# An SSM batch on one Trainium2 core: turning the B products inside unit 1 and making the V products inside unit 2

## The chip, the core and the metric

The kernel runs on one NeuronCore of a Trainium2 chip. Its engines are TensorE (PE, matmuls and transposes), VectorE (DVE), ScalarE (ACT), GpSimd (POOL) and SyncE (SP, which here issues DMAs). The metric is the device time of one execution in microseconds (us), lower being better. The kernel before takes 2384.48 us, the median of 3 runs.

## What is computed

One inference step of a two-layer trunk, in float32. Layer 0 projects 640 tokens (512 of a prompt, 8 streams of 16) to 4096 columns, runs a diagonal state space model (SSM, "S5") over 96 groups of 16 columns on a part of them, attends to a memory with another part, and projects back. Layer 1 does the same with stick-breaking attention in place of the SSM. Only the SSM matters here:

```python
hn = rms_norm(x, g_pre)
u, gate, mq, mg = _split_proj(hn @ w_in)          # the projection that the SSM is interleaved with
y, h_last = s5_scan(u.reshape(bsz, l, SSM_GROUPS, SSM_GROUP), h0, ...)
# in s5_scan, per group:
bu = einsum('gph,btgh->btgp', b_bar, u_blk)       # inputs to the 64 complex states of a group
_, h_loc = lax.associative_scan(_ssm_combine, (a, bu), axis=1)
hs = h_loc + pows[None] * h_prev[:, None]
y = real(einsum('ghp,btgp->btgh', cmat, hs)) + d32 * u_blk
```

## The kernel before

**The projection.** `w_in` is consumed in 16 chunks of 256 columns, each in 4 units. A unit is 4 blocks of 128 rows of the weight; TensorE makes it in four quarters (`q` = 0 to 3 of `unit_stationary`: two blocks of columns by two halves of the tokens), each 4 times the three matmuls of lines 206 to 208, into PSUM banks 0 to 3. The weights of a unit come by DMA into `RAW`, ScalarE rounds them to the high part `WH` (`split_high`, line 174) and VectorE makes the low part `WL` from both (`split_low`, line 188). There are four slots; ScalarE and VectorE split unit U+2 when they stand at unit U (`ahead`), and a slot is loaded again when TensorE is done with its unit.

**The SSM batch.** Chunks 1 to 12 are made in a hardware loop of 6 iterations. One iteration is one SSM batch: 8 units (x = 0 to 7) and, between them, the SSM work for 16 groups (8 pairs). Each engine runs its own instructions in the written order, so a wait holds everything that stands behind it. In a batch the steps are:

- `turn_c` (TensorE, line 483, ahead of unit 0) turns the C matrices and the states; it waits until VectorE has made the last of the three additions of the batch before (`late`, line 712).
- `tables` with `input_products` (VectorE, after its split at unit 0, lines 648 to 380) makes `BV`, the B matrices times powers of A; the semaphore is `s_bv`.
- `second` (ScalarE, line 591) copies a part of `BV` to `BB`.
- `turn_bv` (TensorE, line 496) turns `BV` with 16 transposes into banks 4 to 7. `copy_wv` (ScalarE, line 598) copies them to `WV`.
- `products_v` (TensorE, line 508) makes the V products, inputs of the scan, from `WV` and `U`, in two parts of 16 small matmuls. `copy_v` (ScalarE, line 606) copies each part to `W` and signals `s_Ve`.
- `products_lags` (TensorE, line 521, ahead of unit 4).
- `first`, `second`, `third`, `fourth` of `ssm_dve` (VectorE, lines 633 to 701, one behind each of its splits at x = 3 to 6) run the scan over 64 columns in six levels, then the streams, and write `HPZ`; the semaphore is `s_hp`. `first` waits for both parts of `s_Ve`.
- `products_y` (TensorE, after unit 7): 16 matmuls on `TZ` (line 531), the wait for `s_hp`, 16 matmuls on `HPZ` (line 536), two transposes (line 542). VectorE adds the three banks to `YS` (line 712, `s_ye`); the next batch's `turn_c` waits for the last.

The lists that set the order are `aux` in `ssm_pe` for TensorE and the lists that `ssm_act` and `ssm_dve` return, whose entry k is run behind the split at unit k (entry 8 after the batch). SyncE's and GpSimd's programs hold the stores of `YS` and the loads of `U` that `copy_v` and `products_v` wait for.

Of the kernel before, what the change touches and what calls it, by code (L numbers as in the profile page):

```python
# [76 lines left out]
def build(nc, io, out, scr):  # L77
# [13 lines left out]
    with ExitStack() as ctx:  # L91
# [43 lines left out]
        at = 0  # L135
# [341 lines left out]
        def ssm_pe(pe, ph, i):  # L477

            def turn_c():
                pe.wait_ge(s_crd, i * 80 + 80)  # L480
                pe.wait_ge(s_ye, i * 3 + 3)
                for k in range(2):
                    pe.transpose(PS[:, 4, k * P:k * P + P], CR[:, k, :], ident[:])
                for k in range(2):
                    ins = pe.transpose(PS[:, 4, 256 + 64 * k:320 + 64 * k],
                                       SR[0:64, :].rearrange("b (m r) -> b r m", r=2)[:, k, :], ident[0:64, 0:64])
                ins.then_inc(s_cT, 1)

            def turn_bv():
                pe.wait_ge(s_bv, i + 2)  # L490
                pe.wait_ge(s_cTe, i + 1)
                pe.wait_ge(s_fTe, i + 1)
                for x in range(4):
                    for j in range(4):
                        r, jj = x // 2, 4 * (x % 2) + j
                        ins = pe.transpose(PS[:, 4 + x, j * P:j * P + P], BV[:, r, jj].rearrange("p s h -> p (s h)"), ident[:])
                ins.then_inc(s_wvT, 1)

            def products_v(part):
                if part == 0:  # L500
                    pe.wait_ge(s_u, i * 128 + 128)
                    pe.wait_ge(s_wve, i * 4 + 4)
                for a in range(2):
                    for j in range(4):
                        jj = 4 * part + j
                        for q in range(2):
                            c = j * NC
                            ins = pe.matmul(PS[q * ST:q * ST + ST, 4 + 2 * a + part, c:c + NC],
                                            WV[:, (a * JB + jj) * P + q * ST:(a * JB + jj) * P + q * ST + ST], U[:, 2 * jj + q, :],
                                            start=(j == 0), stop=True, skip_group_check=True)  # L510
                ins.then_inc(s_V, 1)

            def products_lags():
                pe.wait_ge(s_cp, i + 2)
                pe.wait_ge(s_bb, i + 2)
                pe.wait_ge(s_Ve, i * 2 + 2)
                for a in range(2):
                    for r in range(2):
                        for x in range(4):
                            j = 4 * a + x  # L520
                            ins = pe.matmul(PS[32 * x:32 * x + 32, 4 + a, 0:P], BB[:, r, j].rearrange("p q h -> p (q h)"),
                                            CP[:, r, j, 0:8].rearrange("p k h -> p (k h)"),
                                            start=(r == 0), stop=(r == 1), skip_group_check=True)
                ins.then_inc(s_kd, 1)

            def products_y():
                pe.wait_ge(s_tz, i * 128 + 128)
                pe.wait_ge(s_kde, i + 2)
                for g in range(2 * JB):
                    o = PS[:, 4 + g // 6, (g % 6) * NC:(g % 6 + 1) * NC]  # L530
                    pe.matmul(o, TZ[:, g, :], U[:, g, :], start=(g % 6 == 0), stop=False, skip_group_check=True)
                pe.wait_ge(s_hp, i + 2)
                for j in range(JB):
                    o = PS[:, 4 + j // 3, (j % 3) * 2 * NC:(j % 3 + 1) * 2 * NC].rearrange("p (q c) -> p q c", q=2)
                    for r in range(2):
                        ins = pe.matmul(o, CP[:, r, j, 1:9].rearrange("p k h -> p (k h)"), HPZ[:, r, :, j, :],  # L536
                                        start=False, stop=(r == 1), skip_group_check=True)
                    if j in (2, 5, 7):
                        ins.then_inc(s_y, 1)
                pe.wait_ge(s_fs, i + 1)  # L540
                for r in range(2):
                    ins = pe.transpose(PS[0:72, 7, r * P:r * P + P], FS[:, r].rearrange("p b j -> p (b j)"), ident[:])
                ins.then_inc(s_fT, 1)

            aux = {0: [turn_c], 2: [turn_bv], 3: [lambda: products_v(0)], 4: [products_lags]}
            for x in range(8):
                for f in aux.get(x, ()):
                    f()
                n = i * 2 + 1 + x // 4
                unit_stationary(pe, ph, (i * 2 + 1 + x // 4) * 4 + ph.first + x % 4, x % 4, n,  # L550
                                (lambda q: products_v(1) if q == 2 else None) if x == 3 else None)
            products_y()

        def ssm_sync(sp, i):
# [19 lines left out]
        def ssm_act(act, mine, i):  # L574

            def early():
                act.wait_ge(s_cT, i + 2)
                act.wait_ge(s_cp, i + 1)
                act.wait_ge(s_hp, i + 1)
                act.activation(CTH[:, 0:P], PS[:, 4, 0:P], ACT.Copy)  # L580
                act.activation(CTH[:, P:2 * P], PS[:, 4, P:2 * P], ACT.Copy, scale=-1.0)
                act.activation(CTH[:, 2 * P:384], PS[:, 4, 2 * P:384], ACT.Copy).then_inc(s_cTe, 1)

            def second():
                act.wait_ge(s_zero, 3)

                act.wait_ge(s_bv, i + 2)
                act.wait_ge(s_kd, i + 1)
                for q in range(2):
                    r = slice(q * ST, q * ST + ST)  # L590
                    ins = act.activation(BB[r, :, :, q, :], BV[r, :, :, STEPS - 1, :], ACT.Copy)
                ins.then_inc(s_bb, 1)

            def copy_wv():
                act.wait_ge(s_wvT, i + 2)
                for x in range(4):
                    act.activation(WV[:, x * 512:(x + 1) * 512], PS[:, 4 + x, :], ACT.Copy).then_inc(s_wve, 1)

            def copy_v():  # L600
                for part in range(2):
                    act.wait_ge(s_V, i * 2 + 1 + part)
                    if part == 0:
                        act.wait_ge(s_yst, i * 128 + 128)
                    for a in range(2):
                        ins = act.activation(W[:, a, 4 * part:4 * part + 4, :],
                                             PS[:, 4 + 2 * a + part, 0:4 * NC].rearrange("p (j c) -> p j c", j=4), ACT.Copy)
                    ins.then_inc(s_Ve, 1)

            def lags():  # L610
                act.wait_ge(s_kd, i + 2)
                act.wait_ge(s_kst, i * 16 + 16)
                act.activation(KDS[:], PS[:, 4:6, 0:P], ACT.Copy).then_inc(s_kde, 1)

            def late():
                act.wait_ge(s_fT, i + 2)
                act.wait_ge(s_fst, i * 32 + 32)
                act.activation(FO[0:72, :].rearrange("b (m r) -> b r m", r=2),
                               PS[0:72, 7, 0:2 * P].rearrange("b (r m) -> b r m", r=2), ACT.Copy).then_inc(s_fTe, 1)

            return [early, second, copy_wv, copy_v, lags, None, None, None, late]

        def ssm_dve(dve, mine, i):

# [826 lines left out]
        def _(pe):  # L1451
# [40 lines left out]
            with pe.Fori(0, BATCHES) as i:  # L1492
                ssm_pe(pe, ph, i)
# [88 lines left out]
        def _(act):  # L1582
# [75 lines left out]
            with act.Fori(0, BATCHES) as i:  # L1658
                aux = ssm_act(act, mine, i)
                chunk("in_a", i * 2 + 1, i + 1, aux[0:4])  # L1660
                chunk("in_a", i * 2 + 2, i + 10, aux[4:8])
                aux[8]()
# [519 lines left out]
```

## Time and profile before

| | |
|---|---|
| median of 3 runs | 2384.48 us (2380.51 to 2387.82) |
| the profiled execution | 2382.36 us |
| its span | 2380.7 us |
| TensorE busy | 2270.9 us (95%) |
| VectorE, ScalarE, GpSimd busy | 1015.0, 872.3, 290.7 us |
| the loop of 6 SSM batches | from about 155 to 605 us of the span |

Times in the rows below are microseconds from the start of the span. A timeline row has the start, how long the group lasted, the engine, line, operation, what it writes and reads, and how many instructions; in brackets stands how long the engine had been idle before it and who ended the wait.
### The profile page before, as it was taken

To read this page: it belongs to the slowest core of one execution; us is meant where nothing else is said; L and a number is where in the kernel's file an instruction comes from. 1 tells how busy PE (TensorE), PEld (TensorE's weight loads), DVE (VectorE), ACT (ScalarE), POOL (GpSimd) and SP (SyncE) were. 2 spreads that over 40 slices of the span, in tenths; PEclk is the share of its full clock that TensorE was granted. 3 is DMA by queue.
4 is the path that set the end of the run, shared out by engine and by line. 5 is a ranking of instruction groups with operands and counts; after the bars stand their busy time and mean duration, and the time that the engine had idled before them with its cause. 6 is when DMAs were issued, how large, how long until landed. Compare 5 with 4: busy or idle time off the path is not lost.

```text
span 2380.7 us, 36018 instructions
## 1 busy us (share of the span) xinstructions
PE 2270.9 (95%) x13890; PEld 2042.3 (86%) x13890; DVE 1015.0 (43%) x1775; ACT 872.3 (37%) x1596; POOL 290.7 (12%) x580
## 2 busy tenths in 40 slices
PE   8999999999799999999999999999999999889997
PEld 6799999999788998887888889888988888878886
DVE  5658888988534362225222221222212223543223
ACT  4542333323345352224222223544455444442221
POOL 1422120220101000002000000121121211010001
PEclk9999999999899999999999999999999999999998
DMA  7634433433534334223233234334343345244223
GB/s 258 220 81 114 109 103 91 118 102 104 202 117 140 107 105 160 79 80 150 93 102 101 94 100 135 109 107 150 98 139 108 111 147 205 88 151 160 79 79 133
DMA packets 177834, 293.45 MB, mean 123 GB/s; under 512 B 25524, under 2 KB 105056, under 8 KB 174304
## 3 DMA queue, kind: packets, MB, share of 16 engines
q1 hardware_dynamic: 132720, 159.32, 22.3%
q0 software_dynamic: 24304, 88.99, 12.0%
q10 hardware_dynamic: 20736, 44.11, 5.1%
q8 instruction: 51, 0.84, 0.1%
q14 instruction: 23, 0.19, 0.0%
HBM read 243.75 MB, written 48.61 MB: 123 GB/s over the span
## 4 chain that ended last, share of the span: by engine, by line
PE 76%; DVE 9%; DMA 5%; issue 4%; ACT 4%; POOL 1%; ACTq 0%; SPq 0%; POOLq 0%; DVEq 0%
PE PS L1349 11%; PE PS L1351 11%; PE PS L1350 11%; PE PS L206 10%; PE PS L208 10%; PE PS L207 10%; DMA FA<-in_cache_k_dram 2%; DVE WL L188 2%; PE PS L536 2%; DVE FA L643 1%; PE PS L1131 1%; DVE FA L639 1%; PE PS L793 1%; DVE FA L634 1%; PE PS L1116 1%
## 5 line engine op out<-in xcount | busy, mean ns | idle before, releaser
L206 PE MATMUL PS<-XH,WH 128*128 128x320 f32 x2336 | 741.3, 317 | 4.9 <-ACT EST L1639 2.1
L207 PE MATMUL PS<-XL,WH 128*128 128x320 f32 x2336 | 724.9, 310 | 0.0
L208 PE MATMUL PS<-XH,WL 128*128 128x320 f32 x2336 | 724.9, 310 | 0.0
L188 DVE SCALAR_TENSOR_TENSOR WL<-RAW,vec,WH 128x256 fp32r<-128x256 f32 (+1 forms) x608 | 283.6, 527 | 631.8 <-ACT WH L174 627.3
L1349 PE MATMUL PS<-WH,XH 128*128 128x512 f32 x1168 | 456.7, 391 | 7.6 <-DVE WL L183 4.5
L1351 PE MATMUL PS<-WH,XL 128*128 128x512 f32 x1168 | 455.4, 390 | 0.0
L1350 PE MATMUL PS<-WL,XH 128*128 128x512 f32 x1168 | 455.3, 390 | 0.0
L206 PEld LDWEIGHTS PS<-XH,WH 128*128 128x128 f32 x2336 | 442.0, 189 | 13.7 <-issue 5.9
L207 PEld LDWEIGHTS PS<-XL,WH 128*128 128x128 f32 x2336 | 442.0, 189 | 3.1 <-issue 2.9
L208 PEld LDWEIGHTS PS<-XH,WL 128*128 128x128 f32 x2336 | 441.4, 189 | 0.0
L174 ACT ACTIVATE WH<-RAW,vec 128x256 fp32r<-128x256 f32 (+1 forms) x608 | 281.4, 532 | 374.9 <-DMA RAW<-in_w_kv_dram 177.0
L183 DVE TENSOR_TENSOR WL<-RAW,WH 128x1024 fp32r<-128x1024 f32 (+1 forms) x120 | 141.6, 1182 | 339.4 <-ACT WH L170 339.1
L1349 PEld LDWEIGHTS PS<-WH,XH 128*128 128x128 f32 x1168 | 220.0, 188 | 54.6 <-DVE WL L183 5.7
L1351 PEld LDWEIGHTS PS<-WH,XL 128*128 128x128 f32 x1168 | 219.7, 188 | 45.9
L1350 PEld LDWEIGHTS PS<-WL,XH 128*128 128x128 f32 x1168 | 220.0, 188 | 45.6
L170 ACT ACTIVATE WH<-RAW 128x1024 fp32r<-128x1024 f32 (+1 forms) x120 | 121.6, 1016 | 337.2 <-DMA RAW<-in_w_out_b_dram 132.3
L1639 ACT ACTIVATE EST<-PS 128x320 f32<-128x320 f32 x116 | 49.8, 439 | 126.5 <-PE PS L208 126.0
L1177 POOL TENSOR_SCALAR_AFFINE_SELECT FA<-FA 128x128 f32<-128x128 f32 x120 | 30.5, 291 | 364.8 <-DVE FA L1243 246.3
L1445 POOL TENSOR_SCALAR rstd<-ss 128x1 f32<-128x1 f32 x20 | 5.9, 296 | 479.6 <-DVE ss L1931 396.5
L1243 DVE SCALAR_TENSOR_TENSOR FA<-PS,FA 128x512 f32<-128x512 f32 x36 | 22.6, 684 | 97.3 <-ACT FA L1210 97.3
L439 POOL DMA_DIRECT2D FA<-scratch_lags x48 | 26.6, 563 | 201.7 <-DMA scratch_lags<-FA 201.7
L1721 ACT ACTIVATE FA<-PS 128x512 f32<-128x512 f32 x40 | 23.9, 598 | 71.0 <-PE PS L1538 36.1
(309 smaller groups left out, 2133.9 us busy)
## 6 DMA issues: line engine op xcount, KB each, us to landing
RAW<-in_w_in_a_dram SPq DMA_DIRECT2D x64, 512.0 KB, 4.0
RAW<-in_w_in_b_dram SPq DMA_DIRECT2D x64, 512.0 KB, 3.6
RAW<-in_w_kv_dram SPq DMA_DIRECT2D x48, 512.0 KB, 3.6
RAW<-in_w_out_a_dram SPq DMA_DIRECT2D x32, 512.0 KB, 3.8
RAW<-in_w_out_b_dram SPq DMA_DIRECT2D x32, 512.0 KB, 3.8
scratch_in_a<-EST ACTq DMA_DIRECT2D x32, 320.0 KB, 3.7
RAW<-in_w_glu_dram SPq DMA_DIRECT2D x24, 384.0 KB, 3.3
scratch_in_b<-EST ACTq DMA_DIRECT2D x26, 320.0 KB, 4.1
```

Source lines behind the costliest of these rows:

```text
L170: eng.activation(WH[:, slot, 0:n], RAW[:, slot, 0:n], ACT.Copy).then_inc(s_wh, 1)
L174: ins = eng.activation(wview(WH, slot, ph)[:, kt, :], wview(RAW, slot, ph)[:, kt, :], ACT.Copy, scale=vec[:, g:g + 1])
L183: eng.tensor_tensor(WL[:, slot, 0:n], RAW[:, slot, 0:n], WH[:, slot, 0:n].bitcast(F32), ALU.subtract).then_inc(s_wl, 1)
L188: ins = eng.scalar_tensor_tensor(out=wview(WL, slot, ph)[:, kt, :], in0=wview(RAW, slot, ph)[:, kt, :], scalar=vec[:, g:g + 1], in1=wview( ...
L206: pe.matmul(acc, wh, xh, start=first, stop=False)
L207: pe.matmul(acc, wh, xl, start=False, stop=False)
L208: return pe.matmul(acc, wl, xh, start=False, stop=last)
L536: ins = pe.matmul(o, CP[:, r, j, 1:9].rearrange("p k h -> p (k h)"), HPZ[:, r, :, j, :], start=False, stop=(r == 1), skip_group_check=True)
L1349: pe.matmul(PS[:, bank + t, :], xh, wh[:, kt, :], start=first, stop=False)
L1350: pe.matmul(PS[:, bank + t, :], xh, wl[:, kt, :], start=False, stop=False)
L1351: ins = pe.matmul(PS[:, bank + t, :], xl, wh[:, kt, :], start=False, stop=last)
L1639: act.activation(EST[:, m, h * HALF:h * HALF + HALF], PS[:, q, 0:HALF], ACT.Copy).then_inc(s_ev[name], 1)
```

## The change

TensorE's steps: `turn_bv` moves from ahead of unit 2 into unit 1, ahead of its last quarter. The two parts of `products_v` move from ahead of unit 3 and ahead of the third quarter of unit 3 into unit 2, ahead of its third and of its last quarter. ScalarE's steps: `copy_wv` follows at once on the copy of `BB` (behind the split at unit 1), and `copy_v` stands behind the split at unit 2 and not at unit 3. Nothing is added or removed.

```diff
-            aux = {0: [turn_c], 2: [turn_bv], 3: [lambda: products_v(0)], 4: [products_lags]}
+            aux = {0: [turn_c], 4: [products_lags]}
+            inside = {(1, 3): turn_bv, (2, 2): lambda: products_v(0), (2, 3): lambda: products_v(1)}
+
+            def at(x):
+                return lambda q: inside[x, q]() if (x, q) in inside else None
+
             for x in range(8):
                 for f in aux.get(x, ()):
                     f()
                 n = i * 2 + 1 + x // 4
-                unit_stationary(pe, ph, (i * 2 + 1 + x // 4) * 4 + ph.first + x % 4, x % 4, n,
-                                (lambda q: products_v(1) if q == 2 else None) if x == 3 else None)
+                unit_stationary(pe, ph, (i * 2 + 1 + x // 4) * 4 + ph.first + x % 4, x % 4, n, at(x))
...
                 ins.then_inc(s_bb, 1)
-
+                copy_wv()
...
-            return [early, second, copy_wv, copy_v, lags, None, None, None, late]
+            return [early, second, copy_v, None, lags, None, None, None, late]
```

On TensorE the 16 transposes of `BV` stood, before, at a unit's start: the wait for `weights_high` behind them is that of unit 2. (Lines are 4 higher behind the edited place in the changed kernel.)

```order
L208 MATMUL PS<-XH,WL 128x320
L490 REGISTER_ALU
L491 REGISTER_ALU [waits bv_ready]
L496 MATMUL PS<-ident,FA 128x128 [waits finals_copied,c_copied]
L496 MATMUL PS<-ident,FA 128x128 x15
L1314 REGISTER_ALU
L206 MATMUL PS<-XH,WH 128x320 [waits weights_high,weights_low]
```

After, they stand between two quarters of unit 1, whose matmuls go on with no wait of their own:

```order
L208 MATMUL PS<-XH,WL 128x320
L490 REGISTER_ALU
L491 REGISTER_ALU [waits bv_ready]
L496 MATMUL PS<-ident,FA 128x128 [waits finals_copied,c_copied]
L496 MATMUL PS<-ident,FA 128x128 x15
L206 MATMUL PS<-XH,WH 128x320
L207 MATMUL PS<-XL,WH 128x320
```

One quarter of a unit, 12 matmuls, has moved from ahead of the transposes to behind them.

On ScalarE, before, from the copy of `BB` (line 591) to the V copies (line 606); `weights_loaded0` is the split of unit 4, `weights_loaded1` that of unit 5:

```order
L591 ACTIVATE FA<-FA 64x16x16 [waits lags_product,bv_ready,zeros_set]
L591 ACTIVATE FA<-FA 64x16x16
L167 ISA
L174 ACTIVATE WH<-RAW,vec 128x256 [waits weights_loaded0]
L174 ACTIVATE WH<-RAW,vec 128x256 x3
L598 ACTIVATE FA<-PS 128x512 [waits wv_turned]
L598 ACTIVATE FA<-PS 128x512 x3
L174 ACTIVATE WH<-RAW,vec 128x256 [waits weights_loaded1]
L174 ACTIVATE WH<-RAW,vec 128x256 x3
L604 ISA [waits v_products]
L606 ACTIVATE FA<-PS 128x320 [waits y_stored]
```

And after, the same stretch and its end (591 is now 595, 598 is 602, 606 is 610):

```order
L595 ACTIVATE FA<-FA 64x16x16
L602 ACTIVATE FA<-PS 128x512 [waits wv_turned]
L602 ACTIVATE FA<-PS 128x512 x3
L167 ISA
L174 ACTIVATE WH<-RAW,vec 128x256 [waits weights_loaded0]
L174 ACTIVATE WH<-RAW,vec 128x256 x3
L608 ISA [waits v_products]
L610 ACTIVATE FA<-PS 128x320 [waits y_stored]
...
L610 ACTIVATE FA<-PS 128x320 [waits v_products]
L610 ACTIVATE FA<-PS 128x320
L174 ACTIVATE WH<-RAW,vec 128x256 [waits weights_loaded1]
L174 ACTIVATE WH<-RAW,vec 128x256 x3
```

The split of unit 5 now stands behind the V copies, and the split of unit 4 behind the copies of `WV`. VectorE's order is unchanged: split of unit 4, split of unit 5, then `first`.

## Rows read from the trace of the kernel before

**Rows 1.** The page: busy time, share of the span and instructions by engine.

```profile
PE 2270.9 (95%) x13890; PEld 2042.3 (86%) x13890; DVE 1015.0 (43%) x1775; ACT 872.3 (37%) x1596; POOL 290.7 (12%) x580
```

**Rows 2.** TensorE's waits: line, awaited, us in total, times, longest.

```profile
PE PS L536 <- DVE FA L696: 8.8, 6, 1.5
```

**Rows 3.** Timeline of TensorE in the second batch (about 230.5 to 305.6 us).

```profile
230.57 0.44 PE L483 MATMUL PS<-ident,FA 128*128 128x128 f32 x2 [0.36 <-DVE FA L712]
...
243.74 0.31 PE L206 MATMUL PS<-XH,WH 128*128 128x320 f32 x1
...
245.50 1.91 PE L496 MATMUL PS<-ident,FA 128*128 128x128 f32 x16
...
254.38 1.33 PE L508 MATMUL PS<-FA 128*64 128x80 f32 x32
...
259.35 1.33 PE L508 MATMUL PS<-FA 128*64 128x80 f32 x32
...
264.33 1.08 PE L521 MATMUL PS<-FA 128*32 128x128 f32 x32
...
293.60 3.69 PE L531 MATMUL PS<-FA 128*128 128x80 f32 x32
...
298.77 1.62 PE L536 MATMUL PS<-FA 128*128 128x160 f32 x7 [1.47 <-DVE FA L696]
...
305.64 0.44 PE L483 MATMUL PS<-ident,FA 128*128 128x128 f32 x2 [0.36 <-DVE FA L712]
```

**Rows 4.** Timeline of VectorE in the same batch.

```profile
252.25 3.26 DVE L188 SCALAR_TENSOR_TENSOR WL<-RAW,vec,WH 128x256 fp32r<-128x256 f32 x8
261.53 0.68 DVE L633 TENSOR_TENSOR FA<-FA 128x504 f32<-128x504 f32 x1 [6.02 <-ACT FA L606]
...
298.41 0.30 DVE L696 COPY FA<-FA 64x64 f32<-64x64 f32 x2
...
302.50 0.65 DVE L712 TENSOR_TENSOR FA<-FA,PS 128x480 f32<-128x480 f32 x1
...
305.09 0.49 DVE L712 TENSOR_TENSOR FA<-FA,PS 128x320 f32<-128x320 f32 x1 [0.43 <-PE PS L536]
```

**Rows 5.** Timeline of ScalarE in the same batch.

```profile
242.42 0.84 ACT L591 ACTIVATE FA<-FA 64x256 f32<-64x256 f32 x2 [7.74 <-issue]
...
247.45 2.07 ACT L598 ACTIVATE FA<-PS 128x512 f32<-128x512 f32 x4 [2.44 <-PE PS L496]
249.69 1.71 ACT L174 ACTIVATE WH<-RAW,vec 128x256 fp32r<-128x256 f32 x4 [0.17 <-DMA RAW<-in_w_in_a_dram]
...
260.73 0.77 ACT L606 ACTIVATE FA<-PS 128x320 f32<-128x320 f32 x2 [4.12 <-PE PS L508]
```

**Rows 6.** Stretches of 1 us: busy time by engine, PEclk, DMA share, GB/s.

```profile
299.00:300.00 1.00, 1.00 (x7) 1.00 (x7) 0.87 (x3) 0.00 (x0) 0.00 (x0) 0.72 0.00 0
300.00:301.00 1.00, 1.00 (x6) 1.00 (x5) 0.88 (x2) 0.00 (x0) 0.00 (x0) 0.50 0.00 0
...
302.00:303.00 1.00, 1.00 (x6) 1.00 (x6) 1.00 (x3) 0.00 (x0) 0.00 (x0) 0.58 0.00 0
```

**Rows 7.** Two waits elsewhere: a timeline row of TensorE, and stretches of 2 us.

```profile
1570.33 1.63 PE L1101 MATMUL PS<-ident,FA 128*128 128x128 f32 x13 [1.87 <-DMA FA<-in_cache_k_dram]
...
1570.00:1572.00 2.00, 1.67 (x15) 1.68 (x16) 0.00 (x0) 1.99 (x4) 1.41 (x2) 1.00 1.04 367
...
616.00:618.00 2.00, 0.00 (x0) 0.00 (x0) 0.00 (x0) 0.00 (x0) 2.00 (x4) 0.72 0.71 232
```

**Rows 8.** First batch: the copy of BB, and TensorE at the last quarter of unit 1.

```profile
168.42 0.84 ACT L591 ACTIVATE FA<-FA 64x256 f32<-64x256 f32 x2 [6.71 <-issue]
...
168.68 0.31 PE L206 MATMUL PS<-XH,WH 128*128 128x320 f32 x1
```

**Rows 9.** Second batch: stores of YS on SyncE's queue, loads of U on GpSimd's.

```profile
232.44 4.52 SPq L570 DMA_DIRECT2D scratch_y<-FA  x8
...
231.30 4.87 POOL L431 DMA_DIRECT2D FA<-scratch_in_a  x8 [26.04 <-DVE FA L712]
```

## The prediction, as written before the run

> **What bounds the kernel now.** I read the page first. TensorE is busy 95% of the span [rows 1], so only what keeps it idle, or slows its clock, can be won. The table of TensorE's waits comes next: 8.8 us in 6 times for the states, where line 536 waits for VectorE's last write of `HPZ` [rows 2]; that is once in every batch, 1.47 us each. Then the timelines of the second batch, which stands for all six: one batch takes 75.07 us (from the `turn_c` at 230.57 to that at 305.64 [rows 3]), and the others repeat it to within 0.1 us.
>
> The reader should follow one chain backwards there. TensorE finishes the 16 `TZ` matmuls at 293.60+3.69 = 297.29 and starts on `HPZ` at 298.77 [rows 3], because VectorE ended line 696 at 298.41+0.30 = 298.71 [rows 4]. From 261.53 to there VectorE works without a gap of note: scan, splits, streams. It started at 261.53 after 6.02 us of idling, released by ScalarE's second V copy [rows 4], which had started at 260.73 when TensorE finished the second part of the V products, begun at 259.35 [rows 3, 5]. So the scan's length is fixed, and its start is set by where the V products stand in TensorE's order.
>
> The last view is the clock. Right behind that wait the granted clock falls to 0.50, that is from 2.4 to 1.2 GHz. In the four stretches from 299 to 303 us it is 0.72, twice 0.50, and 0.58 [rows 6]; full speed is back at 303. What is missing from full clock in them is 0.28+0.50+0.50+0.42 = 1.70 us, all of it in the `HPZ` matmuls, which TensorE runs without a gap. It is the only fall in a batch, and the other five batches show it at the same place. A batch therefore loses about 1.5 us to the wait and 1.7 us to what follows from it.
>
> **The change part by part.** A quarter of a unit takes (245.50-243.74) = 1.76 us [rows 3]. The number and size of TensorE's instructions is the same, so its own work is zero either way; what changes is when each result is there.
>
> Turn of B: from 245.50 to 243.74. It needs `BV`, and ScalarE's copy, which waits for the same semaphore, started at 242.42 [rows 5]: 1.3 us to spare. In the first batch it is 168.42 against 168.68, 0.26 us to spare [rows 8]. So I cost the added wait at nothing; the cover is that slack, and whatever eats more than it is paid by TensorE one for one, with all later units behind it. ScalarE behind it: the copies of `WV` end at 247.45+2.07-1.76 = 247.8, then the split of unit 4 (1.71 us) at 249.5. VectorE wants that split only at 252.25 [rows 4]: free.
>
> V products: the first part needs `WV` (247.8) and stands ahead of the third quarter of unit 2. With the transposes the last quarter of unit 1 begins at about 245.5, unit 2 at 247.3, its third quarter at 250.9: 3 us to spare. It needs `U` too, whose loads are issued from 231.30 to 236.2, and the V copy needs the `YS` stores, issued until 237.0 [rows 9]; both are over ten microseconds ahead. The second part moves over three quarters, 5.28 us, from 259.35 to 254.07.
>
> The scan's start: not all of the 5.28 us arrives. Before, the split of unit 5 was long made on both engines (ScalarE 249.69, VectorE in the 8 instructions from 252.25). Now ScalarE makes it behind the V copies, and VectorE's `first` stands behind its half of that split. So: second copy at 260.73-5.28 = 255.45, done 0.77 later at 256.2; ScalarE's split 1.71, until 257.9; VectorE's split, 3.26/2 = 1.63, until 259.6. Against 261.53 that is 1.9 us earlier, out of 5.28. It covers the 1.47 us wait with about 0.4 us over: `HPZ` is ready at 296.8, TensorE wants it at 297.3. The load of unit 5 goes out when unit 1 ends, now at 247.3 and not 245.5; it landed at 249.69 before, so 251.5 now, and is not wanted before 256.2. TensorE needs unit 5 after 272 us. None of the later splits moves: they hang on units 3 and later, whose times stand still, and VectorE reaches them later than ScalarE has them ready.
>
> What is late next: `HPZ` matmuls start at 297.3. The three additions of VectorE follow. The first stood, without a gap, at 302.50 [rows 4]; 1.9 earlier it is 300.6, and with two of some 0.6 us each the third could start at 301.8. The third waits for the last matmul, though: at 305.09 before, minus 1.5 and minus 1.7 is 301.9. So the two are about level, and `turn_c` moves from 305.64 to about 302.4. The 0.36 us wait there stays. Everything of the next batch hangs on that point, with its slacks unchanged, and the steps after the last batch too.
>
> The wait is worth 1.47 us. How much of the 1.70 us of clock comes back is the unknown. Bounds: nothing, if the short matmuls on `TZ` (80 columns each, 3.69 us) are what makes it fall; all, if the wait is. Speaking for the wait: of the other falls in this trace none stands in a stretch that TensorE filled, each comes right behind or in one in which it idled, like that at 616 us, where it did nothing for 2 us and the clock was down to 0.72 [rows 7]. Against it being that simple: in layer 1 TensorE idled for 1.87 us ahead of line 1101 and the clock stayed at 1.00 [rows 7]. So a wait of this size alone does not always do it, which means that the light work around it may count. But without the wait nothing in this trace is known to do it. I take all of it, and keep both ends.
>
> In the Trainium skill, "TensorE: Matmul & The Clock Gate", section "What's actually happening", the gate follows how busy TensorE has lately been, not waits as such. By that rule the wait and the thin stretch ahead of it are added up, so taking away one of them may not be enough; the sum would then be that of rival 1. By that rule, the trace agrees so far as every fall is behind idling, and no row here shows the thin stretch without a wait.
>
> One more price could lie in breaking up units. Before, the first part of the V products stood at a unit's boundary and the second inside a unit. From the first to the second, and from there to the lags at 264.33, TensorE took 4.97 and 4.98 us [rows 3], each with two quarters in it: inside costs the same as at the boundary. The skill says, in the same page under "Step-by-step: what each phase is for", that TensorE pulls weight loads ahead of running matmuls, so a wait in the middle of a unit might stop that. By that rule each of the three places would pay one weight load, 2042.3/13890 = 0.147 us on average [rows 1], in all 18 x 0.147 = 2.6 us, and the forecast would stand at 2368.1; the pair above shows none of it.
>
> Sum: 6 batches x (1.47 + 1.70) = 19.0 us. The profiled execution would go from 2382.36 to 2363.4, and the median from 2384.48 to 2365.5.
>
> **The rivals.**
>
> 1. The wait goes, the clock falls all the same, on the short `TZ` matmuls. Then 6 x 1.47 = 8.8 us: 2375.7. For it: the thin stretch stays, and the idling of 1.87 us that left the clock at 1.00 [rows 7]. Against: no fall in this trace without idling. 12%.
>
> 2. The scan does not start early enough. VectorE's `first` waits for a split that now waits for the V copies; if ScalarE's chain costs 1.5 us more than I think (a late `RAW`, a store that holds the copy), the scan starts 0.4 us earlier only, the wait stays at 1.1 us and the clock falls as before. Then 6 x 0.4 = 2.4 us: 2382.1, no measurable change. This is the case in which the change does not do what it says. Against: each term is a duration of the trace. 8%.
>
> 3. The B products are not there at three quarters of unit 1. The place is TensorE's wait for `s_bv`. `BV` would have to come later than now by the slack of 1.3 us and by more. A wait of w there delays units, V products and the end of the batch by w; it is slower than before only if w eats the 3.2 us won. If it lowers the clock itself (1.7 us) that point is w = 1.5 us, so `BV` 2.8 us late. At w = 2.5 with its own fall the balance is +1.0 us a batch: 2390.5. Against: nothing ahead of `BV` moves against `turn_c`. 4%.
>
> 4. A part only: VectorE's additions become the bound, or some batches keep the wait. 8 to 15 us: about 2373. 6%.
>
> **How the numbers follow.** The forecast has 70%, the rivals 12, 8, 4 and 6%. A measurement of this kernel can tell 0.3% from no change, 7.2 us, its runs spread by that much. Faster by more: 70+12+5 = 87%. Within: 9%. Slower: 4%. Low end: 6 x (1.6 + 1.8 + 0.36) = 22.6, if the matmuls close up wholly and the wait ahead of `turn_c` goes too, and 3 us for the spread: 2359. High end: rival 1 with 1 us of spread: 2377.
>
> **What would show it.** In the changed kernel the wait of line 536's matmuls (now 540) on VectorE should be gone from the table or under 0.1 us. A batch should last 71.9 us. The scan's first instruction should start 1.9 us earlier against `turn_c`, the granted clock should read 1.00 from the first batch to the last, and no wait should stand ahead of the transposes of `BV`. If the batch lasts 73.6 us and the clock still falls, it was rival 1. If the scan starts less than 1.5 us earlier, it was rival 2 and my chain of copy, split and split is wrong. The forecast would be wrong altogether if TensorE waits at line 491.

## The result

The changed kernel takes 2362.15 us (median of 6 runs, 2357.86 to 2367.49), the kernel before 2382.8 us in the runs beside it (6 runs, 2375.78 to 2387.82): ratio 0.9917, 95% interval 0.9896 to 0.9938. That is 20.7 us less; 19.0 were forecast.

### The profile page after: what moved, and what is told of

It reads as the page before. It is cut to its first block, busy times and chain, and to the rows that moved or that the text cites. A ratio compares the mean times of both kernels' runs of the same rounds, so it can differ in the third digit from the quotient of the medians.

```text
span 2359.7 us, 36018 instructions
## 1 busy us (share of the span) xinstructions
PE 2257.7 (96%) x13890; PEld 2031.2 (86%) x13890; DVE 1015.2 (43%) x1775; ACT 873.1 (37%) x1596; POOL 291.9 (12%) x580
## 2 busy tenths in 40 slices
DMA packets 177834, 293.45 MB, mean 124 GB/s; under 512 B 25524, under 2 KB 105056, under 8 KB 174304
## 4 chain that ended last, share of the span: by engine, by line
PE 84%; DMA 6%; ACT 4%; DVE 2%; issue 2%; POOL 1%; SPq 0%; ACTq 0%; POOLq 0%
PE PS L206 13%; PE PS L207 12%; PE PS L208 12%; PE PS L1353 11%; PE PS L1355 11%; PE PS L1354 11%; DMA FA<-in_cache_k_dram 3%; PE PS L536 1%; PE PS L1135 1%; PE PS L797 1%; PE PS L531 1%; PE PS L1120 1%; PE PS L1105 1%; ACT XH L1058 1%; PE PS L826 1%
```

## The profile after

The loop of the six batches as one stretch, from the first `turn_c` to the first matmul behind the loop, before and after (columns: length, busy time and count for PE, PEld, DVE, ACT, POOL, granted clock, DMA share, GB/s):

```profile
155.56:606.14 450.58, 439.33 (x3398) 429.53 (x3397) 380.94 (x756) 135.13 (x332) 77.69 (x131) 0.98 0.40 106
```

```profile
155.27:585.61 430.34, 427.92 (x3398) 419.03 (x3396) 380.82 (x756) 135.86 (x332) 77.91 (x131) 1.00 0.42 111
```

Of the 21.0 us that the profiled execution's span lost (2380.7 to 2359.7), 450.58-430.34 = 20.2 are in the loop. The instructions are the same in number; TensorE is busy 439.33-427.92 = 11.4 us less with them, as the clock is 1.00 and not 0.98, and idles (450.58-439.33)-(430.34-427.92) = 8.8 us less.

TensorE in the second batch of the changed kernel, as in rows 3:

```profile
226.90 0.44 PE L483 MATMUL PS<-ident,FA 128*128 128x128 f32 x2 [0.36 <-DVE FA L716]
...
240.07 1.91 PE L496 MATMUL PS<-ident,FA 128*128 128x128 f32 x16
...
247.19 1.33 PE L508 MATMUL PS<-FA 128*64 128x80 f32 x32
...
250.40 1.33 PE L508 MATMUL PS<-FA 128*64 128x80 f32 x32
...
289.93 3.69 PE L531 MATMUL PS<-FA 128*128 128x80 f32 x32
293.45 4.55 PE L536 MATMUL PS<-FA 128*128 128x160 f32 x32
297.84 0.38 PE L542 MATMUL PS<-ident,FA 128*72 128x128 f32 x2
298.59 0.44 PE L483 MATMUL PS<-ident,FA 128*128 128x128 f32 x2 [0.36 <-DVE FA L716]
```

The batch lasts 298.59-226.90 = 71.69 us, against 75.07 in rows 3. The row of line 536 has no bracket any more, and its matmuls start 293.45-289.93 = 3.52 us behind the first `TZ` matmul, against 298.77-293.60 = 5.17: the wait was worth 1.65 us. From their start to line 542 they take 297.84-293.45 = 4.39 us and not 304.89-298.77 = 6.12: the clock was worth 1.73. The end of that stretch in the kernel before:

```profile
304.89 0.38 PE L542 MATMUL PS<-ident,FA 128*72 128x128 f32 x2
```

No row of lines 496 or 508 has a bracket: the moved steps wait for nothing.

VectorE, as in rows 4:

```profile
248.58 1.67 DVE L188 SCALAR_TENSOR_TENSOR WL<-RAW,vec,WH 128x256 fp32r<-128x256 f32 x4
254.16 1.67 DVE L188 SCALAR_TENSOR_TENSOR WL<-RAW,vec,WH 128x256 fp32r<-128x256 f32 x4 [3.91 <-ACT WH L174]
255.74 0.68 DVE L637 TENSOR_TENSOR FA<-FA 128x504 f32<-128x504 f32 x1
...
292.68 0.31 DVE L700 COPY FA<-FA 64x64 f32<-64x64 f32 x2
...
296.77 1.76 DVE L716 TENSOR_TENSOR FA<-FA,PS 128x480 f32<-128x480 f32 x3
```

And ScalarE, as in rows 5:

```profile
238.75 0.84 ACT L595 ACTIVATE FA<-FA 64x256 f32<-64x256 f32 x2 [7.74 <-issue]
242.01 2.07 ACT L602 ACTIVATE FA<-PS 128x512 f32<-128x512 f32 x4 [2.41 <-PE PS L496]
244.11 1.71 ACT L174 ACTIVATE WH<-RAW,vec 128x256 fp32r<-128x256 f32 x4
...
251.77 0.77 ACT L610 ACTIVATE FA<-PS 128x320 f32<-128x320 f32 x2 [2.36 <-PE PS L508]
252.42 1.70 ACT L174 ACTIVATE WH<-RAW,vec 128x256 fp32r<-128x256 f32 x4
```

The scan starts 255.74-226.90 = 28.84 us behind `turn_c`; before it was 261.53-230.57 = 30.96. That is 2.1 us earlier. The bracket at 254.16 shows what took the rest of the 5.3 us by which the second V copy is earlier (251.77-226.90 = 24.87 against 260.73-230.57 = 30.16): VectorE stood 3.91 us before the split of unit 5, because ScalarE made its half (252.42) behind the V copies. `HPZ` is ready at 292.68+0.31 = 292.99, 0.46 us before TensorE reaches it. The three additions now follow each other without a gap, as the prediction had them, level with TensorE.

The clock where it had fallen (the same stretch of the batch as rows 6):

```profile
294.00:295.00 1.00, 1.00 (x10) 1.00 (x9) 1.00 (x1) 0.00 (x0) 0.00 (x0) 1.00 0.42 164
295.00:296.00 1.00, 1.00 (x10) 1.00 (x9) 0.88 (x4) 0.00 (x0) 0.00 (x0) 1.00 0.00 0
```

## The experiments

What was open: whether the wait or the thin `TZ` matmuls (80 columns each) lowered the clock, which of the moves was needed, how much cover the turn of B had, and whether a better order was close to the change. "Batch" below is the distance of two `turn_c` from the second on, which repeats within 0.1 us in each trace (within 0.2 with four additions, below) and so tells differences that the 0.3% of the whole time doesn't. Part of that 0.3% is the clock elsewhere: added up over stretches of 1 us, what is missing from full clock outside the loop comes to 28.3 us in the traces of the kernel before and of the changed one alike, but to 33.4 us in that of the smallest edit below and to 21.8 in that of both small edits, although all edits lie inside the loop.

### The wait kept and filled

Edit of the kernel before, behind the matmuls of line 531. The results of the six extra matmuls go into a part of bank 7 that nothing reads:

```diff
+                for g in range(6):
+                    pe.matmul(PS[:, 7, 256 + 0:256 + NC], TZ[:, g, :], U[:, g, :], start=True, stop=True, skip_group_check=True)
                 pe.wait_ge(s_hp, i + 2)
```

> The kernel before, with 6 extra matmuls on TZ (into a spare part of bank 7, read by nobody) behind the 16 of line 531, so that TensorE works while it waits for HPZ. The wait is kept, only its idling is filled. My theory, that the idling is what lowers the clock: the HPZ matmuls start where they did (about 68.2 us after turn_c), the granted clock stays at 1.00 and they take 4.4 us and not 6.1, a batch lasts 73.3 to 73.5 us and not 75.07, the whole 9 to 11 us less than before. Rival, that the thin stretch of small matmuls lowers it: the clock still falls behind them, a batch lasts 75.0 us, no change.

Measured 2372.46 us (10 runs), ratio 0.9967 (0.9956 to 0.9979). Its second batch:

```profile
292.05 3.69 PE L531 MATMUL PS<-FA 128*128 128x80 f32 x32
295.57 1.50 PE L533 MATMUL PS<-FA 128*128 128x80 f32 x12
297.24 4.61 PE L538 MATMUL PS<-FA 128*128 128x160 f32 x32 [0.16 <-DVE FA L698]
301.69 0.38 PE L544 MATMUL PS<-ident,FA 128*72 128x128 f32 x2
302.63 0.44 PE L483 MATMUL PS<-ident,FA 128*128 128x128 f32 x2 [0.56 <-DVE FA L714]
```

and the stretch of these matmuls in it:

```profile
297.00:302.00 5.00, 4.84 (x35) 4.55 (x34) 4.72 (x12) 0.00 (x0) 0.00 (x0) 1.00 0.00 1
```

Line 538 (536 before) starts 68.2 us behind `turn_c`, as before the edit, but the clock is 1.00 and it is through after 301.69-297.24 = 4.45 us. The batch is 73.62 us. Useless matmuls, of the same shape as the thin ones ahead of them, won 1.45 us a batch, 8.7 us in six (the medians differ by 7.6). So at this place it is the idling that brings the fall on; the thin matmuls alone do not. Whether they help it was not tested, as no run put other work ahead of the wait. The fall alone is worth 1.7 us, of which 0.2 went into a longer wait for the additions (0.56 for 0.36 us).

### How long a wait lowers it

The changed kernel with k extra additions on VectorE ahead of the copies to `HPZ` (k = 2, 3, 4; `k` stands for the number in each run):

```diff
                 dve.wait_ge(s_zero, 3)
+                for x in range(k):
+                    d = FA[:, 19904 + 512 * x:19904 + 512 * x + 504].rearrange("p (j c) -> p j c", j=JB)
+                    tt(d, W[:, 0, :, 0:63], W[:, 1, :, 0:63], ALU.add)
```

> The changed kernel with 2 extra additions of 128x504 on VectorE (about 0.59 us each, into unused memory) ahead of the copies to HPZ, so that HPZ is ready 1.2 us later. The slack there is 0.4 us, so TensorE should idle 0.8 us at the HPZ matmuls (the profile's idle time, counted from the end of the matmul before, about 0.6). Theory: a wait that short leaves the clock at 1.00 in all six batches, a batch lasts 72.5 us. Rival (any wait behind the small matmuls lowers it): clock at 0.50 behind it, 74.2 us.

> As late2 with 3 extra additions, HPZ 1.8 us later, 1.4 us of wait (profile about 1.2), a little less than the 1.65 (1.47) of the kernel before. Theory: this is near the size at which the clock falls; it falls in some or all batches, 73.1 us for a batch without a fall and 74.8 with one. Rival (something else of the old order lowered the clock): 1.00 throughout.

> As late2 with 4 extra additions, HPZ 2.4 us later, 2.0 us of wait, more than in the kernel before. Theory: the clock falls in every batch, a batch lasts 75.4 us, so the loop gives back more than the change won (22 us over the changed kernel). Rival: 1.00 throughout, 73.7 us a batch.

| k | time (1 run) | idle at line 536 | batch | clock behind it |
|---|---|---|---|---|
| 2 | 2376.27 us | 0.57 to 0.60 us | 72.7 us | 1.00 in all six |
| 3 | 2374.48 us | 1.17 to 1.19 us | 73.3 us | 1.00 in all six |
| 4 | 2389.08 us | 1.76 to 1.78 us | 75.2 to 75.4 us | falls in all six |
| kernel before | 2384.28 us beside them (1 run; the other columns are from the trace of rows 3) | 1.47 us | 75.07 us | falls in all six |

Two rows of TensorE and a stretch, with three additions:

```profile
298.49 4.61 PE L536 MATMUL PS<-FA 128*128 128x160 f32 x32 [1.17 <-DVE FA L703]
302.94 0.38 PE L542 MATMUL PS<-ident,FA 128*72 128x128 f32 x2
...
297.00:303.00 6.00, 4.83 (x36) 4.66 (x36) 5.70 (x17) 0.00 (x0) 0.00 (x0) 1.00 0.22 82
```

and with four:

```profile
302.32 6.29 PE L536 MATMUL PS<-FA 128*128 128x160 f32 x32 [1.77 <-DVE FA L703]
308.45 0.38 PE L542 MATMUL PS<-ident,FA 128*72 128x128 f32 x2
...
302.00:308.00 6.00, 5.67 (x29) 5.68 (x30) 4.86 (x13) 0.00 (x0) 0.00 (x0) 0.72 0.00 0
```

0.6 us more of waiting made the same 16 instructions 1.7 us longer. I had thought that three additions might be enough in some batches, and they were not in any. The single times of k = 2 and 3 can't be told apart; their batches can.

A threshold between 1.17 and 1.47 us of idle time does not follow, though. The fall does not keep its distance to the wait. In the run with four additions it begins about 0.6 us behind the end of the wait in the first batch, and ahead of that end in the sixth, where the clock is 0.51 from 603 us on and the matmuls start at 603.47:

```profile
226.96 6.29 PE L536 MATMUL PS<-FA 128*128 128x160 f32 x32 [1.78 <-DVE FA L703]
603.47 6.05 PE L536 MATMUL PS<-FA 128*128 128x160 f32 x32 [1.78 <-DVE FA L703]
...
227.00:228.00 1.00, 1.00 (x6) 1.00 (x7) 0.87 (x4) 0.00 (x0) 0.00 (x0) 0.78 0.00 0
603.00:604.00 1.00, 0.53 (x2) 0.53 (x3) 0.84 (x8) 0.00 (x0) 0.00 (x0) 0.51 0.00 0
```

And the wait in layer 1 that rows 7 show with 1.87 us and a full clock recurs in every trace, behind the same instructions. With four additions it is 1.92 us long and the clock falls behind it; in the trace of the changed kernel taken again (the last section of the experiments) it is 2.15 us long and the clock stays:

```profile
1574.49 1.80 PE L1108 MATMUL PS<-ident,FA 128*128 128x128 f32 x13 [1.92 <-DMA FA<-in_cache_k_dram]
1576.00:1577.00 1.00, 1.00 (x6) 1.00 (x5) 0.30 (x1) 0.67 (x2) 0.00 (x0) 0.50 0.90 303
...
1546.15 1.63 PE L1105 MATMUL PS<-ident,FA 128*128 128x128 f32 x13 [2.15 <-DMA FA<-in_cache_k_dram]
1547.00:1548.00 1.00, 1.00 (x11) 1.00 (x9) 0.00 (x0) 1.00 (x3) 0.07 (x1) 1.00 0.84 291
```

So the length of a wait alone does not decide whether the clock falls, and the moment of a fall is not set by the end of the wait. What else decides it is not shown. Each of these kernels has one trace, and its six batches are near copies of each other, so six out of six is less than six independent trials.

### TensorE's part alone

`copy_wv` and `copy_v` stay where they were in ScalarE's order:

```diff
-                copy_wv()
...
-            return [early, second, copy_v, None, lags, None, None, None, late]
+            return [early, second, copy_wv, copy_v, lags, None, None, None, late]
```

> The change on TensorE alone; ScalarE keeps the order of before (split of unit 4 ahead of the WV copies, split of unit 5 ahead of the V copies). Theory (only the states' readiness at the HPZ matmuls counts, and the split of unit 5 is what held back 3.2 of the 5.3 us): the scan starts 5.0 to 5.3 us earlier against turn_c than before (25.7 to 26.0 us behind it, in place of 28.8 in the changed kernel), yet a batch lasts 71.7 us as in the changed kernel, and the whole is within 1 us of it. Rival (a longer lead of VectorE is worth something): a batch under 71.5 us. Rival (ScalarE's order is needed): TensorE waits for WV ahead of the V products.

Measured 2358.07 us (4 runs), ratio 0.9908 (0.9889 to 0.9927), batch 71.69 us. The scan starts 254.77-229.09 = 25.68 us behind `turn_c`, 5.3 us earlier than before (VectorE's rows, and TensorE's at line 536):

```profile
250.77 3.26 DVE L188 SCALAR_TENSOR_TENSOR WL<-RAW,vec,WH 128x256 fp32r<-128x256 f32 x8
254.77 0.68 DVE L636 TENSOR_TENSOR FA<-FA 128x504 f32<-128x504 f32 x1 [0.74 <-ACT FA L609]
...
292.43 0.30 DVE L699 COPY FA<-FA 64x64 f32<-64x64 f32 x2
...
295.65 4.55 PE L536 MATMUL PS<-FA 128*128 128x160 f32 x32
```

All of the 5.28 us arrive with ScalarE's old order, and none of the 3.2 us more than in the changed kernel is worth anything: the batch is that of the changed kernel to 0.01 us. So ScalarE's half of the change is not needed. It made the scan later than it had to be, and left 0.46 us of cover where 2.9 were to be had: here `HPZ` is ready at 292.43+0.30 = 292.73 and TensorE reaches it at 295.65.

### The smallest edit that covers the wait

On the kernel before, `turn_bv` and ScalarE as they were; only the second part of the V products is moved:

```diff
-            aux = {0: [turn_c], 2: [turn_bv], 3: [lambda: products_v(0)], 4: [products_lags]}
+            aux = {0: [turn_c], 2: [turn_bv], 3: [lambda: products_v(0), lambda: products_v(1)], 4: [products_lags]}
...
-                                (lambda q: products_v(1) if q == 2 else None) if x == 3 else None)
+                unit_stationary(pe, ph, (i * 2 + 1 + x // 4) * 4 + ph.first + x % 4, x % 4, n)
```

> The kernel before with one edit: both parts of the V products stand ahead of unit 3, so the second is two quarters (3.5 us) earlier; B is turned where it was and ScalarE's order is that of before. Theory: the scan starts 3.5 us earlier than before (27.4 us behind turn_c), which covers the 1.65 us; the wait and the fall of the clock go, a batch lasts 71.7 us, the whole is 20 to 21 us less than before, as the full change. Rival (turning B inside unit 1 or breaking up units is part of the gain): a batch longer than 71.8 us.

Measured 2359.6 us (4 runs), ratio 0.9906 (0.9888 to 0.9925). The wait and the fall are gone and the scan starts 27.09 us behind `turn_c`. The batch is 71.35 us, though, and not 71.7: 0.34 us less than with the full change. A row of TensorE shows where (against 247.19 and 250.40 above):

```profile
252.62 2.44 PE L508 MATMUL PS<-FA 128*64 128x80 f32 x64
254.99 0.41 PE L206 MATMUL PS<-XH,WH 128*128 128x320 f32 x1
```

One group of 32 matmuls takes 2.44 us where two of 16 take 1.33 each. These durations overlap the rows behind them; over the batch the joined group saves 0.34 us. Whether the joining or the boundary did it was asked next.

### Joined, but inside a unit

The changed kernel, with `(2, 2): lambda: (products_v(0), products_v(1))`:

> The changed kernel with both parts of the V products ahead of the third quarter of unit 2, B still turned inside unit 1. It tells why v_together had batches 0.34 us shorter than the changed kernel. Theory 1, each separate group of small matmuls costs some 0.34 us for itself, and joining two saves that wherever they stand: 71.35 us. Theory 2, it was standing inside a unit that cost it (three places inside against none): 71.6 to 71.7 us here.

One run, 2358.92 us; batch 71.35 us. The second group of small matmuls costs some 0.34 us for being a group of its own, at the boundary and inside a unit alike; breaking up a unit costs nothing beyond that. What makes up the 0.34 us is not shown.

### The turn of B one quarter earlier

The changed kernel with `(1, 2): turn_bv`:

> The changed kernel with B turned one more quarter earlier, at half of unit 1. BV is then late: the slack of 1.3 us less a quarter of 1.76 us is -0.45 us, and 0.26-1.76 = -1.5 us in the first batch. Theory (that slack is all the cover there is, paid one for one beyond): TensorE waits 0.4 to 0.5 us at the transposes of BV in five batches and 1.5 us in the first, a batch lasts 72.1 to 72.2 us, the whole 3 to 4 us more than the changed kernel. Rival (TensorE's queue hides it): no wait, 71.7 us.

One run, 2369.76 us, batches of 72.27 to 72.35 us, the first 73.31. TensorE's waits:

```profile
PE PS L496 <- DVE FA L380: 3.6, 6, 1.5
```

The wait came as the slack said: 1.50 us in the first batch, 0.39 to 0.47 in the others. The batch grew by 0.6 us, more than these, because the profile counts idle time from the end of the matmul before, which overlaps the next by some 0.16 us when nothing waits. The same makes the 1.47 us of rows 3 into 1.65.

### The wait ahead of turn_c

The changed kernel, where `turn_c` writes to bank 4 only, which the first addition reads:

```diff
                 pe.wait_ge(s_crd, i * 80 + 80)
-                pe.wait_ge(s_ye, i * 3 + 3)
+                pe.wait_ge(s_ye, i * 3 + 1)
```

> The changed kernel, with turn_c waiting for the first of VectorE's three additions (the one that reads bank 4, into which it writes) and not for the third. Theory: the 0.36 us wait ahead of turn_c goes in five of the six batches, the transposes start right behind those of line 542, a batch lasts about 71.3 us, 2 us less than the changed kernel in all. VectorE's B work hangs on its own additions and on ScalarE, which is 0.4 us earlier too, so the slack ahead of the turn of B stays near 1.3 us. Rival (VectorE's additions come late enough to hold the split of unit 2 and BV, so that TensorE waits at the turn of B instead): slack under 1 us and no gain.

Measured 2358.02 us (5 runs), ratio 0.9905 (0.9889 to 0.9921), batch 71.11 us: 0.58 us less than the changed kernel, more than the 0.36 of idle time, again by the overlap:

```profile
296.98 4.55 PE L536 MATMUL PS<-FA 128*128 128x160 f32 x32
301.37 0.38 PE L542 MATMUL PS<-ident,FA 128*72 128x128 f32 x2
301.59 0.38 PE L483 MATMUL PS<-ident,FA 128*128 128x128 f32 x2
```

What I expected of the slack was wrong. ScalarE did not move with `turn_c`, and `BV` hangs on it: VectorE's split ahead of `BV` waits for ScalarE's half.

```profile
304.14 1.67 DVE L188 SCALAR_TENSOR_TENSOR WL<-RAW,vec,WH 128x256 fp32r<-128x256 f32 x4 [2.09 <-ACT WH L174]
```

The split starts 304.14-301.59 = 2.55 us behind `turn_c`; in the changed kernel it was 2.03. ScalarE's copy of `BB` starts 12.4 us behind `turn_c` and no longer 11.9, so some 0.7 us are left of 1.3. It still covers.

### Both small edits

The joined V products on the kernel before, with `turn_c` waiting for one addition; and the changed kernel again beside it.

> The two edits that gave the shortest batches put together, on the kernel before: both parts of the V products joined ahead of unit 3 (batch 71.35 us alone), and turn_c waiting for the first addition only (0.58 us less alone, 71.11 against 71.69). Theory, that they are independent (one is at the middle of the batch, the other at its end): 70.77 us a batch, 6 x 0.92 = 5.5 us less than the changed kernel, about 2356 us on the chip where the changed kernel takes 2362. Rival (the slack ahead of BV's turn, which is 3.1 us here since B is turned ahead of unit 2, or the additions, becomes the bound): 71.1 us.

> The changed kernel once more, on the same chip and beside the same runs of the kernel before as both_edits, for their difference. Expected: 0.991 to 0.992 of the kernel before, 71.69 us a batch, and 5 to 6 us more than both_edits.

| | time (6 runs each) | ratio to before | batch |
|---|---|---|---|
| both small edits | 2353.84 us | 0.9888 (0.9873 to 0.9904) | 70.77 us |
| changed kernel again | 2358.46 us | 0.9910 (0.9892 to 0.9928) | 71.69 us |

The two edits add up to the hundredth in the batch: 0.92 us less, 5.5 us in six. The medians differ by 4.6 us and the intervals of the ratios overlap a little, but both were measured beside the same runs of the kernel before, and five of the six runs of the changed kernel are above all six of the other. The batches show the size of the difference in the loop.

## Why the prediction was right

**What bounds the kernel.** Right. The batch lost 75.07-71.69 = 3.38 us, and that is the wait's 1.65 and the clock's 1.73 with nothing left over. Outside the loop the span lost 0.8 us. (The waiting matmuls are still line 536 in the changed kernel, not 540: they stand ahead of the edited place.)

**Turn of B at no cost.** Right in all six batches, the first with its 0.26 us included. The cover is real and no larger than it was said to be: another quarter earlier, TensorE waits 0.39 to 1.50 us at the transposes.

**The chain to the scan's start.** Forecast 1.9 us earlier, measured 2.1; neighbouring rows overlap a little, and I had put them end to end. That the split of unit 5 holds back some 3 us was right: with TensorE's part alone, where that split stands ahead of the V copies, the whole 5.3 us arrive.

**The wait.** 1.47 us in the sum, 1.65 in fact: the term was taken from the idle time, which is counted from the end of the last matmul. The row of `TZ` matmuls had the rest in it: 32 records in 3.69 us, each 0.275 us long, so they follow each other at (3.69-0.275)/31 = 0.11 and overlap by 0.165.

**The clock.** 1.70 in the sum, 1.73 measured. That all of it comes back was the choice with the least behind it. I had seen that falls follow idling, while the 1.87 us of rows 7 spoke against it; `fill` has now shown it for this place. With waits near the size of this one, whether the clock falls is not settled by their length, as the same wait in layer 1 shows, so a wait made only somewhat shorter would not have been sure to give the clock back. In the Trainium skill, "TensorE: Matmul & The Clock Gate", section "What's actually happening", the gate goes by how busy TensorE has been lately. By that rule the trace of `fill` agrees: the matmuls that kept the clock up did nothing useful.

**Breaking up units.** The pair of rows was read rightly, as inside costing the same as at the boundary, but that was half of the question. Both places in that pair paid for being a group of their own, 0.34 us, and joining the two groups would have saved it. The change made no use of that, and it added no group, so the sum did not suffer. The price of 0.147 us for each place inside a unit did not come either: nothing of the 3.38 us is missing for it.

**The rivals.** None came. Rival 1 fell with the clock at 1.00 in all six batches, rival 2 with the scan's start, rival 3 only appears when B is turned a quarter earlier, and of rival 4 the additions did become level with TensorE, but `turn_c` waits for them 0.36 us as before. Forecast 71.9 us for a batch, measured 71.69. The 1.3 us by which six batches gave more than the sum are the two terms' 0.18 and 0.03 us a batch; the rest of the difference between 19.0 and 20.7 us lies outside the loop and within the spread of the runs.

## What to carry to other kernels

A short wait on TensorE can cost twice its length when the clock falls behind it, so look at the granted clock in stretches of 1 us behind each repeated wait, and price both. When a result is late, look which step in the waiting engine's own order stands between the result and its use: moving the producer by 5.3 us brought 2.1 here, as a split had been put behind the copies on ScalarE. And ask for the smallest move that covers the wait: once it is covered, more lead is worth nothing, while each separate group of small matmuls between large ones costs something.

## What was not expected of the hardware

The same 16 instructions of line 536 take 4.4 us behind 1.17 us of idle time and 6.1 behind 1.47 or 1.77: the clock is either lowered or not. But a wait's length does not tell which: at one and the same place in layer 1 the clock fell behind 1.92 us of idle time in one trace and stayed at 1.00 behind 2.15 us in another, and a fall can begin before the wait is over. A second group of 16 small matmuls between large ones costs some 0.34 us that joining it to the first saves. Idle time in front of a matmul, as the profile has it, is about 0.16 to 0.2 us less than what removing the wait gives back.
